# ScalarE issues the down loads of experts 1 to 28 on its own queue, in place of SyncE

## The chip, the core and the metric

One core of a Trainium2 chip runs the whole kernel. The time is the device time of one execution in microseconds (us), from start to end; of several runs the median counts. The engines are TensorE (PE; PEld is its weight load), VectorE (DVE), ScalarE (ACT), GpSimd (POOL) and SyncE (SP). SyncE, ScalarE and GpSimd can issue transfers, each on a queue of its own: in the profile q1 is SyncE's, q10 ScalarE's, q0 GpSimd's. All queues are served by the same 16 transfer engines.

## The reference, cut to what matters

The reference is one layer of a hybrid encoder on 272 tokens (16 meta tokens and a sequence of 256), with a model width of 1024, in float32. First comes a mixer of two kinds of attention (not touched here), then a mixture of 32 experts, of which each token takes 4:

```
gu = xb @ w_gate_up[e] + b_gate_up[e]                 # 1024 x 2048 per expert
act = x_glu * sigmoid(1.702 * x_glu) * (x_lin + 1)    # both halves clamped at 7
yb = act @ w_down[e] + b_down[e]                      # 1024 x 1024 per expert
out[token] += gate * yb
```

A final norm is applied, and the 256 tokens of the sequence are the output. Every expert has tokens, so all expert weights are read: 8.4 MB of gate and up rows and 4.2 MB of down rows for each of 32 experts, 403 MB in all.

## The kernel before, in words

**Loads and slots.** The mixer takes the first 250 us. The experts follow in one pass (more passes are possible if an expert has more than 64 tokens). An expert's weights come in three loads of 4 MB: two for the gate and up matrix (four of eight row groups each) and one for the down matrix. The 96 loads of a pass have numbers 0 to 95. There are four slots of 4 MB in SBUF, two in the tensor `arena` and two in `ring`; load n goes to slot n mod 4 (`eslot`, L413). The order of the numbers is that of use by TensorE: gate and up of expert 0 (loads 0, 1), gate and up of expert 1 (2, 3), down of expert 0 (4), gate and up of expert 2 (5, 6), down of expert 1 (7), and so on. So the down load of expert x is load 3x + 4, and its slot was last used by load 3x, the second gate and up load of expert x.

**Who issues them.** SyncE issues every load, in the order of the numbers. Loads 0 to 3 go ahead, while the mixer still ends. Before every other load it waits until TensorE has used its slot: TensorE adds 1 to the semaphore `wide_used` of the slot after each quarter of a load, and `slot_free` (L483) waits for all four. Loads 4 to 11 (`first_refill`, L487) go in quarters of 1 MB, each as soon as its own quarter of the slot is used. Loads 12 to 92 are whole (`whole_load`, L495): 12 to 83 in a loop of 6 turns of 12 loads, then one by one. Loads 93 to 95 (`last_loads`, L500) go in quarters again, of load 95 only the first half, since the other half (`kept`) was loaded long before. A load that lands adds 16 to `wide_loaded` of its slot; of a quartered load the last quarter does so, and the first three add to `part_loaded`.

**TensorE.** It waits in `arrived` (L1676) for the load, and for loads 4 to 11 also for `part_loaded`. It works in pairs of experts (`expert_pair`, L1738): gate and up products of the odd expert (L1696), with the transposes of the expert before it between the two loads (L1673), the transpose of the gated pick (L1706), the down products of the even expert (L1712), the scatter into PSUM (L1732), for the next pair the gather of its tokens (L1600), then the same with the next even expert's gate and up and the odd expert's down rows, without a gather. The last pair is written out (`last_pair`, L1776).

**ScalarE.** Its own `expert_pair` (L771) does for each pair: sigmoid; `rows_out` (L749), the copy of the gate and up products out of PSUM, for which it waits with `slot_done` (L396) until TensorE has used the second gate and up load of the expert; `pick_out` (L761), the copy of the gated pick; `down_out` (L766), the copy of the down products; and the same again for the second expert. It issues no loads of expert weights. Its queue carries four small loads near 246 us (L736 to L738) and at the end the store of the second tile (L820), while SyncE stores the first (L571).

Of the kernel before, what the change touches and what calls it, by code (L numbers as in the profile page):

```python
# [65 lines left out]
DN_ROWS = 2 * GU_ROWS  # L66
EWIDTH = GU_ROWS * 2 * D
ESLOT = 2 * NSLOT * SLOT // EWIDTH
GU_LOADS = CH // GU_ROWS
# [5 lines left out]
UNROLL = 2  # L75
# [4 lines left out]
REFILL_END = 3 * ESLOT  # L80
LOAD_TURNS = (PASS_LOADS - ESLOT - REFILL_END) // TURN_LOADS
BIAS_TURN = 3

LAST_READ = [("mid", 2)] * 2 + [("ka", 1), ("ka", 3), ("qa", 1), ("qa", 3)] + [("va", 2)] * 2 \
    + [("gate", 2 * m + 1) for m in range(8)] + [("ba", 3)] * 2 + [("bb", 3)] * 2 \
# [49 lines left out]
def build(nc, x, meta, w_in, b_forget, w_uq, w_uk, w_uv, w_qidx, kln_g, kln_b, w_a, w_b, w_out,  # L135
# [10 lines left out]
    with ctx:  # L146
# [254 lines left out]
        def cols(first, n):  # L401

            return slice(first, first + n) if isinstance(first, int) else bass.ds(first, n)
# [9 lines left out]
        def eslot(k):  # L413

            home, n = divmod(k % ESLOT, ESLOT // 2)
            return (ring if home else more)[:, n * EWIDTH:(n + 1) * EWIDTH]
# [23 lines left out]
        def _(sp):  # L440
# [45 lines left out]

            def first_refill(base):  # L487

                for idx in range(ESLOT, REFILL_END):
                    for q in range(QUARTERS):  # L490
                        sp.wait_ge(wide_used[idx % ESLOT], base + QUARTERS * (idx // ESLOT - 1) + q + 1)
                        quarter_of(idx, rows_of(idx - GU_LOADS, 1), q,
                                   wide_loaded[idx % ESLOT] if q == QUARTERS - 1 else part_loaded[idx % ESLOT])

            def whole_load(idx, base, e0):  # L495

                slot_free(idx, base)
                sp.dma_start(eslot(idx), rows_of(idx - GU_LOADS, e0)).then_inc(wide_loaded[idx % ESLOT], 16)
# [13 lines left out]
            def whole_pass(b):  # L512

                base = b * (QUARTERS * PASS_USES)
                if not isinstance(b, int):
                    base = sp.snap(base)
                first_refill(base)
                with sp.Fori(0, LOAD_TURNS) as j:
                    turn = j * (QUARTERS * TURN_USES) + base
                    if not isinstance(b, int):  # L520
                        turn = sp.snap(turn)
                    for o in range(TURN_LOADS):
                        whole_load(REFILL_END + o, turn, j * (2 * UNROLL) + 1)
                for idx in range(REFILL_END + LOAD_TURNS * TURN_LOADS, PASS_LOADS - ESLOT):
                    whole_load(idx, base, 1)
                last_loads(base)

# [77 lines left out]
        def _(sc):  # L605
# [143 lines left out]
            def rows_out(tb, o, home):  # L749

                slot_done(sc, tb, o)
                sc.activation(gl.rearrange("q (b j p) -> q b j p", p=P, j=DN_ROWS),  # L752
                              banks(home, home + 2).rearrange("q (b p j) -> q b j p", p=P, j=DN_ROWS),
                              ACT.Copy).then_inc(s_gl, 1)

            def sigmoid(x):

                sc.wait_ge(s_glu, x + 1)
                sc.activation(sg, glu, ACT.Sigmoid, scale=1.702).then_inc(s_sig, 1)  # L759

            def pick_out(x, home):  # L761

                sc.wait_ge(s_pgf, x + 1)
                sc.activation(pickgT, bank[home][:, 0:2 * P], ACT.Copy).then_inc(s_pgt, 1)
# [3 lines left out]
                slot_done(sc, tb, o)  # L768
                sc.activation(yr, bank[1], ACT.Copy).then_inc(s_y, 1)  # L769

            def expert_pair(tb, u, last):  # L771
                a = tb * (2 * UNROLL) + 2 * u
                o = 2 * EXPERT_LOADS * u
                sigmoid(a)
                rows_out(tb, o + 1, 2)
                pick_out(a, 7)
                if last:
                    sigmoid(a + 1)
                down_out(tb, o + 2)
                if not last:  # L780
                    sigmoid(a + 1)
                    rows_out(tb, o + 4, 2)
                pick_out(a + 1, 0 if last else 7)
                down_out(tb, o + 3 if last else o + 5)

            with sc.Fori(0, n_pass) as b:
                rows_out(sc.snap(b * TURNS), -1, 6)
                sc.wait_ge(s_btf, b + 1)
                sc.activation(biasT[:].rearrange("p (h n) -> p h n", h=2),
                              banks(0, 2).rearrange("p (h n) -> p h n", h=2)[:, :, 0:CH * EXPERTS],  # L790
                              ACT.Copy).then_inc(s_bT, 1)
                with sc.Fori(0, BIAS_TURN) as j:
                    tb = sc.snap(b * TURNS + j)
                    for u in range(UNROLL):
                        expert_pair(tb, u, False)
                sc.wait_ge(s_gzf, b + 1)
                sc.activation(gT, bank[1][0:EXPERTS, 0:2 * P], ACT.Copy).then_inc(s_gT, 1)
                with sc.Fori(BIAS_TURN, TURNS - 1) as j:
                    tb = sc.snap(b * TURNS + j)
                    for u in range(UNROLL):  # L800
                        expert_pair(tb, u, False)
                tb = sc.snap(b * TURNS + (TURNS - 1))
                expert_pair(tb, 0, False)
                expert_pair(tb, 1, True)
# [454 lines left out]
        def _(pe):  # L1259
# [416 lines left out]
            def arrived(tb, o):  # L1676

                idx = GU_LOADS + o
                pe.wait_ge(wide_loaded[idx % ESLOT], tb * (16 * TURN_USES) + 16 * (idx // ESLOT + 1))
                if ESLOT <= idx < REFILL_END and parts[0] is not None:  # L1680
                    pe.wait_ge(part_loaded[idx % ESLOT], parts[0] + 48 * (idx // ESLOT))

            def gate_up(tb, o, e, home, fresh, between):

# [48 lines left out]
                                 yr[n * CAP:(n + 1) * CAP, :], start=True, stop=True)  # L1733
                    ins.then_inc(s_sc, 1)

            ahead, parts = [None], [None]

            def expert_pair(tb, u):  # L1738
                g = tb * UNROLL + u
                x = tb * (2 * UNROLL) + 2 * u  # L1740
                o = 2 * EXPERT_LOADS * u

                def first_features():

                    pe.wait_ge(s_pkg, g + 1)
                    features(x)

                def second_features():

                    pe.wait_ge(s_acc[0], x + 1)  # L1750
                    features(x + 1)

                gate_up(tb, o, 1, 2, None, first_features)
                pick_rows(x, 0)
                down(tb, o + 2, x)
                scatter(x)
                pe.wait_ge(s_pick, g + 1)
                gather(0)
                gather(1)
                gate_up(tb, o + 3, 0, 2, g * 2 + 2, second_features)  # L1760
                for t in range(2):
                    pe.wait_ge(s_acc[t], x + 1)
                pick_rows(x + 1, 1)
                down(tb, o + 5, x + 1)
                scatter(x + 1)
# [60 lines left out]
            with pe.Fori(0, n_pass) as b:  # L1826
                x = pe.snap(b * EXPERTS)
                ahead[0] = pe.snap(b * 16 + 16)
                fine = pe.snap(b * (48 * (REFILL_END // ESLOT - 1)))
                gate_up(pe.snap(b * TURNS), -GU_LOADS, 0, 6, x, None)  # L1830
                pe.wait_ge(s_bias, 32)
                bias_features()
                parts[0] = fine
                with pe.Fori(0, BIAS_TURN) as j:
                    tb = pe.snap(b * TURNS + j)
                    for u in range(UNROLL):
                        expert_pair(tb, u)
                parts[0] = None
                for t in range(2):
                    ins = tr(bank[1][0:EXPERTS, t * P:(t + 1) * P], gz[:, t, :], ident)  # L1840
                ins.then_inc(s_gzf, 1)
                pe.wait_ge(s_bdn, 16)
                for t in range(2):
                    pe.wait_ge(s_acc[t], x + 4 * BIAS_TURN)
                pe.wait_ge(s_gT, b + 1)
                for t in range(2):
                    for n in range(2):
                        ins = mm(bank[4 + 2 * t + n], gT[:, t * P:(t + 1) * P], bdn[:, n * 512:(n + 1) * 512],
                                 start=True, stop=True)
                    ins.then_inc(s_bm, 1)  # L1850
                with pe.Fori(BIAS_TURN, TURNS - 1) as j:
                    tb = pe.snap(b * TURNS + j)
                    for u in range(UNROLL):
                        expert_pair(tb, u)
                tb = pe.snap(b * TURNS + (TURNS - 1))
                expert_pair(tb, 0)
                last_pair(tb, b)
                for t in range(2):
                    pe.wait_ge(s_acc[t], x + EXPERTS)
                    pe.wait_ge(s_ba[t], b + 1)  # L1860
# [51 lines left out]
```

## Time and profile before

| | us |
|---|---|
| median of three runs | 1174.15 (1173.03 to 1175.33) |
| profiled execution | 1176.58 |
| its span, from the first to the last instruction | 1174.8 |
| TensorE busy | 1109.2 (94%) |
| VectorE busy | 336.3 (29%) |
| ScalarE busy | 206.3 (18%) |
| GpSimd busy | 14.5 (1%) |
| share of the 16 transfer engines taken by q1 | 87.4% |
| share taken by q0, by q10 | 0.6%, 0.4% |

A busy share is over the whole span. The strips of the page cut the span into 40 slices of 29.4 us. The chain that ended last is given as 67% TensorE and 27% transfers. A whole load's median time from issue to landing is between 27.7 and 29.8 us by kind; this is queueing and transfer together.

### The profile page before, as it was taken

The page shows a single profiled execution, that of the slowest core. Times are in us where ns is not written, and L with a number is a line of the kernel's source. Part 1 is how long each engine was busy: PE and PEld are TensorE (multiplying, and loading weights), DVE is VectorE, ACT ScalarE, POOL GpSimd, SP SyncE. Part 2 cuts the span into 40 slices and gives each one's busy share as a digit, 9 for nine tenths or more (in the row PEclk, how much of TensorE's full clock was granted, in tenths as well). Part 3 has the DMA queues.
Part 4 walks back from the last instruction along what each step waited for, and adds up shares of the span by engine and source line. Part 5 has one row for each costly group of instructions (what it writes and reads, how often), then busy time and mean ns, then how long its engine had stood idle before and what let it go on. Part 6 is the DMA issues. An engine that isn't in the chain of part 4 may idle for free.

```text
span 1174.8 us, 13591 instructions
## 1 busy us (share of the span) xinstructions
PE 1109.2 (94%) x5490; PEld 528.0 (45%) x5490; DVE 336.3 (29%) x773; ACT 206.3 (18%) x361; POOL 14.5 (1%) x27
## 2 busy tenths in 40 slices
PE   8999999999999999989899999898989899999897
PEld 6878888553443434333434343334333433343333
DVE  2256442131232222313222322122222222222223
ACT  2437772031001000100000100000000010100012
POOL 3010000000000000000000000000000000000000
PEclk9999999999999999999989999999999999999999
DMA  9813237759999999999999999999999999999992
GB/s 303 279 37 110 106 109 285 322 203 423 421 431 432 433 434 431 430 432 433 434 431 429 429 429 433 436 431 430 431 433 435 431 431 430 432 436 429 432 415 99
DMA packets 39734, 433.66 MB, mean 369 GB/s; under 512 B 3144, under 2 KB 19682, under 8 KB 23188
## 3 DMA queue, kind: packets, MB, share of 16 engines
q1 hardware_dynamic: 38144, 429.45, 87.4%
q0 software_dynamic: 960, 2.30, 0.6%
q10 hardware_dynamic: 596, 1.45, 0.4%
q8 instruction: 23, 0.38, 0.1%
q14 instruction: 11, 0.09, 0.0%
HBM read 432.13 MB, written 1.05 MB: 369 GB/s over the span
## 4 chain that ended last, share of the span: by engine, by line
PE 67%; DMA 27%; DVE 2%; ACT 2%; issue 1%; SPq 0%; ACTq 0%; DVEq 0%
PE psum L1696 24%; PE psum L1712 13%; DMA arena<-in_w_down 12%; DMA ring<-in_w_down 10%; PE psum L1550 4%; PE psum L1600 4%; PE psum L1732 3%; PE psum L1350 2%; PE psum L1529 2%; DMA ring<-in_w_gate_up 2%; DMA arena<-in_w_gate_up 2%; PE psum L1569 2%; PE psum L1673 2%; PE psum L1790 1%; ACT arena L769 1%; PE psum L1310 1%
## 5 line engine op out<-in xcount | busy, mean ns | idle before, releaser
L1696 PE MATMUL psum<-ring,arena 128*64 128x512 f32 x992 | 221.5, 599 | 3.9 <-DMA ring<-in_w_gate_up 3.9
L1696 PE MATMUL psum<-arena 128*64 128x512 f32 x992 | 220.4, 597 | 1.5 <-DMA arena<-in_w_gate_up 1.5
L1193 DVE TENSOR_TENSOR h<-h,psum 128x1024 f32<-128x1024 f32 x64 | 75.3, 1218 | 423.0 <-PE psum L1732 423.0
L1696 PEld LDWEIGHTS psum<-ring,arena 128*64 128x64 f32 x992 | 69.3, 138 | 138.8 <-issue 137.1
L1712 PE MATMUL psum<-ring,arena 128*64 128x512 f32 x528 | 121.9, 615 | 9.6 <-DMA ring<-in_w_down 7.2
L1696 PEld LDWEIGHTS psum<-arena 128*64 128x64 f32 x992 | 68.7, 137 | 135.8 <-issue 132.5
L1712 PE MATMUL psum<-arena 128*64 128x512 f32 x496 | 115.1, 618 | 11.1 <-DMA arena<-in_w_down 11.0
L1173 DVE TENSOR_TENSOR arena<-psum,biasT 128x512 f32<-128x512 f32 x64 | 44.0, 687 | 196.5 <-PE psum L1673 196.5
L759 ACT ACTIVATE arena<-arena 128x512 f32<-128x512 f32 x32 | 20.2, 630 | 413.7 <-DVE arena L1177 413.7
L1732 PE MATMUL psum<-arena 64*128 64x512 f32 x256 | 63.6, 611 | 25.2 <-ACT arena L769 25.2
L1712 PEld LDWEIGHTS psum<-ring,arena 128*64 128x64 f32 x528 | 40.3, 141 | 80.0 <-issue 80.0
L1712 PEld LDWEIGHTS psum<-arena 128*64 128x64 f32 x496 | 35.9, 141 | 79.3 <-issue 69.6
L752 ACT ACTIVATE arena<-psum 128x1024 f32<-128x1024 f32 x32 | 32.8, 1024 | 180.4 <-PE psum L1696 175.2
L1600 PEld LDWEIGHTS psum<-arena 128*128 128x128 f32 x512 | 58.4, 192 | 12.1 <-issue 12.1
L1600 PE MATMUL psum<-arena 128*128 128x128 f32 x512 | 61.4, 278 | 0.0
L1550 PE MATMUL psum<-arena,ring 128*128 128x256 f32 x256 | 60.5, 379 | 0.0
L769 ACT ACTIVATE arena<-psum 128x512 f32<-128x512 f32 x32 | 19.1, 597 | 226.0 <-PE psum L1712 226.0
L1732 PEld LDWEIGHTS psum<-arena 64*128 64x128 f32 x256 | 24.8, 186 | 65.6 <-issue 65.6
L1550 PEld LDWEIGHTS psum<-arena,ring 128*128 128x128 f32 x256 | 46.2, 190 | 5.6
L1673 PEld LDWEIGHTS psum<-kst,arena 128*128 128x128 f32 x256 | 27.4, 141 | 26.1 <-issue 25.2
L836 DVE TENSOR_TENSOR arena<-psum,vT 128x512 f32<-128x512 f32 (+1 forms) x42 | 28.4, 681 | 36.9 <-PE psum L1600 23.7
L1673 PE MATMUL psum<-kst,arena 128*128 128x128 f32 x256 | 35.0, 280 | 0.8 <-ACT arena L752 0.8
(232 smaller groups left out, 767.9 us busy)
## 6 DMA issues: line engine op xcount, KB each, us to landing
arena<-in_w_gate_up SPq DMA_DIRECT2D x29, 4096.0 KB, 29.8
ring<-in_w_gate_up SPq DMA_DIRECT2D x28, 4096.0 KB, 29.8
arena<-in_w_down SPq DMA_DIRECT2D x14, 4096.0 KB, 29.0
ring<-in_w_down SPq DMA_DIRECT2D x13, 4096.0 KB, 27.7
arena<-in_w_gate_up SPq DMA_DIRECT2D x16, 1024.0 KB, 15.4
ring<-in_w_in SPq DMA_DIRECT2D x14, 1024.0 KB, 12.1
ring<-in_w_down SPq DMA_DIRECT2D x14, 1024.0 KB, 16.4
ring<-in_w_gate_up SPq DMA_DIRECT2D x8, 1024.0 KB, 15.4
```

What stands on the lines that cost most here:

```text
L752: sc.activation(gl.rearrange("q (b j p) -> q b j p", p=P, j=DN_ROWS), banks(home, home + 2).rearrange("q (b p j) -> q b j p", p=P, j=DN_ROWS),
L769: sc.activation(yr, bank[1], ACT.Copy).then_inc(s_y, 1)
L836: return v.tensor_tensor(dst, src, vec.unsqueeze(2).broadcast_to([P] + cols), ALU.mult)
L1173: return v.tensor_tensor(dst.rearrange("p (m j) -> p m j", m=8), src, bias[:, m:m + 8, cols(e, 1)].broadcast_to([P, 8, CAP]), ALU.add)
L1193: v.tensor_tensor(half, half, banks(4 + 2 * t, 6 + 2 * t), ALU.add).then_inc(s_acc[t], 1)
L1350: ins = mm(job_bank(name)[:, 0:width], win(s)[:, c, k * P:(k + 1) * P], xnT[:, c, cols:cols + width], start=c == 0, stop=c == CH - 1)
L1550: ins = mm(job_bank(name)[:, 0:SEQ], win(8 + m // 2)[:, c, (m % 2) * P:(m % 2 + 1) * P], xnT[:, c, META:KEYS], start=c == 0, stop=c == CH - 1)
L1600: ins = mm(bank[k][:, c * P:(c + 1) * P], hs[:, t, (4 * k + c) * P:(4 * k + c + 1) * P], pick[:, t, :], start=t == 0, stop=t == 1)
L1673: ins = tr(bank[4 + m // 4][:, (m % 4) * P:(m % 4 + 1) * P], gl[:, m * P:(m + 1) * P], ident)
L1696: ins = mm(bank[home + n][h * CAP:(h + 1) * CAP, :], xg[:, c, e * CAP:(e + 1) * CAP], eslot(idx)[:, (2 * j + h) * D + n * 512:(2 * j + h) ...
L1712: ins = mm(bank[1][n * CAP:(n + 1) * CAP, :], act[:, c * CAP:(c + 1) * CAP], w[:, n * 512:(n + 1) * 512], start=first, stop=last)
L1732: ins = mm(bank[4 + 2 * t + n], pickgT[n * CAP:(n + 1) * CAP, t * P:(t + 1) * P], yr[n * CAP:(n + 1) * CAP, :], start=True, stop=True)
```

## The change

`BY_SCALAR` names loads 7, 10, 13, ... 88: the down loads of experts 1 to 28. SyncE leaves them out wherever it issued them. ScalarE issues each one, whole, right after the `rows_out` that has waited for the last use of its slot. Down loads of experts 0, 29, 30 and 31 stay with SyncE. Since loads 7 and 10 are now whole, the quartered loads of the start (`FINE`) are 4, 5, 6, 8, 9 and 11, and TensorE counts `part_loaded` accordingly. Slots, order of use and semaphores for arrival are the same.

```diff
+LOOP_EXPERTS = 2 * UNROLL * (TURNS - 1)
+BY_SCALAR = [GU_LOADS + EXPERT_LOADS * x + 2 for x in range(1, LOOP_EXPERTS + 1)]
+FINE = [idx for idx in range(ESLOT, REFILL_END) if idx not in BY_SCALAR]
...
-                for idx in range(ESLOT, REFILL_END):
+                for idx in FINE:
...
                     for o in range(TURN_LOADS):
+                        if REFILL_END + o in BY_SCALAR:
+                            continue
                         whole_load(REFILL_END + o, turn, j * (2 * UNROLL) + 1)
                 for idx in range(REFILL_END + LOAD_TURNS * TURN_LOADS, PASS_LOADS - ESLOT):
+                    if idx in BY_SCALAR:
+                        continue
                     whole_load(idx, base, 1)
...
+            def down_load(o, e):
+
+                sc.dma_start(eslot(GU_LOADS + o), w_dn[0, cols(e, 1), :, :].rearrange("e (p j) n -> p (e j n)", j=DN_ROWS)
+                             ).then_inc(wide_loaded[(GU_LOADS + o) % ESLOT], 16)
...
-            def expert_pair(tb, u, last):
+            def expert_pair(tb, u, last, pair=None):
                 a = tb * (2 * UNROLL) + 2 * u
                 o = 2 * EXPERT_LOADS * u
                 sigmoid(a)
                 rows_out(tb, o + 1, 2)
+                if pair is not None:
+                    down_load(o + 5, pair + 1)
                 pick_out(a, 7)
...
                 if not last:
                     sigmoid(a + 1)
                     rows_out(tb, o + 4, 2)
+                    if pair is not None:
+                        down_load(o + 8, pair + 2)
                 pick_out(a + 1, 0 if last else 7)
...
-                        expert_pair(tb, u, False)
+                        expert_pair(tb, u, False, j * (2 * UNROLL) + 2 * u)
...
-                if ESLOT <= idx < REFILL_END and parts[0] is not None:
-                    pe.wait_ge(part_loaded[idx % ESLOT], parts[0] + 48 * (idx // ESLOT))
+                if idx in FINE and parts[0] is not None:
+                    home = [n for n in FINE if n % ESLOT == idx % ESLOT]
+                    pe.wait_ge(part_loaded[idx % ESLOT], parts[len(home) - 1] + 48 * (home.index(idx) + 1))
```

## Rows read from the trace of the kernel before

**Rows 1.** The page: busy tenths of the transfer engines in 40 slices of the span.
```profile
DMA  9813237759999999999999999999999999999992
```

**Rows 2.** Windows: us, busy time (instructions) of each engine, TensorE clock, DMA share, GB/s.
```profile
330.00:475.00 145.00, 141.06 (x706) 56.30 (x706) 39.86 (x64) 14.54 (x22) 0.00 (x0) 1.00 1.01 432
475.00:1150.00 675.00, 628.59 (x3020) 245.49 (x3018) 171.88 (x285) 61.66 (x97) 0.00 (x0) 0.98 1.00 431
```

**Rows 3.** Waits of TensorE, 470 to 1175 us: us in total, times, longest.
```profile
PE psum L1712 <- DMA arena<-in_w_down: 11.0, 5, 2.3
PE psum L1712 <- DMA ring<-in_w_down: 7.2, 4, 2.4
```

**Rows 4.** Timeline of TensorE near the end: start us, length, instruction, idle before it.
```profile
1079.64 7.09 PE L1696 MATMUL psum<-ring,arena 128*64 128x512 f32 x32 [1.66 <-DMA ring<-in_w_gate_up]
1086.65 0.44 PE L1706 MATMUL psum<-kst,arena 128*128 128x128 f32 x2
1089.28 7.09 PE L1712 MATMUL psum<-arena 128*64 128x512 f32 x32 [2.19 <-DMA arena<-in_w_down]
...
1118.51 7.09 PE L1712 MATMUL psum<-ring,arena 128*64 128x512 f32 x32 [0.17 <-DMA ring<-in_w_down]
```

**Rows 5.** Last quarters of loads 6 and 11, load 91: issue, then time to landing.
```profile
L481 SPq DMA_DIRECT2D ring<-in_w_gate_up x1: 328/328/328, 276.0 to 276.0; - x1
...
DMA to landing us min/median/max: 14.0/14.0/14.0
...
L481 SPq DMA_DIRECT2D ring<-in_w_gate_up x1: 328/328/328, 320.4 to 320.4; - x1
...
DMA to landing us min/median/max: 19.3/19.3/19.3
...
L498 SPq DMA_DIRECT2D ring<-in_w_down x1: 328/328/328, 1086.8 to 1086.8; - x1
...
DMA to landing us min/median/max: 31.6/31.6/31.6
```

**Rows 6.** ScalarE's timeline; queues (rows, MB, share) in 246.8 to 249, 249 to 252.
```profile
245.97 2.13 ACT L731 ACTIVATE arena<-h,st 128x1024 f32<-128x1024 f32 x1 [0.23 <-DVE st L1077]
245.97 0.80 ACTq L736 DMA_DIRECT2D arena<-in_b_gate_up  x2
...
q1 hardware_dynamic: 52, 0.85, 90.4%
...
q10 hardware_dynamic: 251, 0.83, 98.3%
```

**Rows 7.** The stores: issues; queues in 1171.2 to 1172.4, then in 1172.5 to 1173.1.
```profile
1170.23 0.39 ACTq L820 DMA_DIRECT2D out<-arena  x1
1170.26 1.00 SPq L571 DMA_DIRECT2D out<-arena  x2
...
1171.42 0.34 ACTq L820 DMA_DIRECT2D out<-arena  x1
...
q10 hardware_dynamic: 114, 0.23, 51.1%
q1 hardware_dynamic: 120, 0.23, 51.1%
...
q1 hardware_dynamic: 112, 0.23, 97.1%
q10 hardware_dynamic: 13, 0.01, 3.9%
```

**Rows 8.** GpSimd's issue; queues in 16 to 18 us, then in 22 to 23.
```profile
14.11 0.58 POOL L584 DMA_DIRECT2D bfor<-in_b_forget  x1 [11.60 <-DMA ring<-in_w_in]
...
q1 hardware_dynamic: 689, 0.70, 110.4%
...
q0 software_dynamic: 73, 0.28, 75.0%
q1 hardware_dynamic: 76, 0.08, 24.1%
```

More of the change, by code:

```diff
@@ L800, in _ @@
                     for u in range(UNROLL):
-                        expert_pair(tb, u, False)
+                        expert_pair(tb, u, False, j * (2 * UNROLL) + 2 * u)
                 tb = sc.snap(b * TURNS + (TURNS - 1))
@@ L1734, in scatter @@
                     ins.then_inc(s_sc, 1)
-            ahead, parts = [None], [None]
+            ahead, parts = [None], [None, None]
             def expert_pair(tb, u):
@@ L1828, in _ @@
                 ahead[0] = pe.snap(b * 16 + 16)
-                fine = pe.snap(b * (48 * (REFILL_END // ESLOT - 1)))
+                fine = [pe.snap(b * (48 * n)) for n in (1, 2)]
                 gate_up(pe.snap(b * TURNS), -GU_LOADS, 0, 6, x, None)
@@ L1832, in _ @@
                 bias_features()
-                parts[0] = fine
+                parts[:] = fine
                 with pe.Fori(0, BIAS_TURN) as j:
```

## The prediction

> **What bounds the kernel now.** First the strip over the span: the transfer engines are full in every slice from the tenth on, to the last but one [rows 1]. The windows say how full: 432 GB/s at a share of 1.01 from 330 to 475 us, 431 GB/s at 1.00 up to 1150, with TensorE busy for 628.6 of the 675 us of the second stretch [rows 2]. A load is 4.194 MB, so it takes 4.194 / 432 = 9.71 us of all engines. TensorE is the smaller load, and what ends its waits is the arrival of down rows, nine times, 18.2 us in all [rows 3]. So from about 260 us to the end of the loads the time is the number of bytes over the rate, as long as the queue never runs dry. Last, the end of the chain: TensorE waits 2.19 us for the down rows of expert 28 (load 88) and begins on them at 1089.28; it meets load 91 at 1118.51 after only 0.17 us of waiting and goes on without a wait for weights to the end of the span at 1174.8 [rows 4]. That start at 1089.28, and the one at 1118.51 behind it, are what the change has to move if it is to move the time; the 56.3 us behind 1118.51 are TensorE, VectorE and the store.
>
> Terms below are against the profiled execution, 1176.58 us (span 1174.8, and 1.8 around it); the median of the runs is 1174.15, so I take the differences found here from the median.
>
> **The change, part by part.**
>
> *Issuing 28 down loads from ScalarE.* SyncE loses 28 issues of 0.33 us, which lay in waits for slots: worth nothing. ScalarE gains 28 issues of 0.34 to 0.39 us [rows 7], some 10 us in all. Each stands behind the copy of the gate and up rows and before the copy of the gated pick. ScalarE's queue can issue while its engine still runs: a load was issued at 245.97, in the same moment in which an activation of 2.13 us began [rows 6]. So the issue fits beside the copy ahead of it. If it did not, the pick copy would come 0.4 us late; it is needed only behind the down products, which take 7.09 us [rows 4], and all that follows on ScalarE waits for TensorE anyway. Bounds 0 and 0.4 us on a step with over 6 us of cover: 0.
>
> *When the load is issued.* Its slot is that of the second gate and up load of the expert in hand, and ScalarE waits for that very use before its copy. SyncE waited for the same event. Moved by 0.1 us or so, with more than two loads outstanding: 0.
>
> *SyncE's order.* It no longer waits for those slots before it goes on to the next load, but the next load's slot comes free later still (it is the slot of the down rows used after). Nothing is issued earlier: 0.
>
> *The first two (loads 7 and 10) whole and not in quarters.* They leave at about 284.1 and 313.1, when the last quarter of the slot is free; before, their first quarters left 5 us sooner. Does the queue run dry meanwhile? The last quarter of load 6 left at 276.0 and landed 14.0 us later, at 290.0 [rows 5]: 5.9 us of work stand ahead at 284.1. The last quarter of load 11 left at 320.4 and landed at 339.7, so five quartered loads took 49.7 us, 9.94 each, and load 9 landed near 319.8: 6.7 us of cover at 313.1. No gap. There is a small gain: 9.94 against 9.71 us is 0.23 us for three boundaries more, or 0.077 us for each; two loads with three boundaries fewer give -0.46 us. Bounds -0.5 and 0; as the queue bounds all that follows, I take -0.4.
>
> *The waits of TensorE* are the same in number or fewer, none on the path.
>
> *Two queues in place of one.* This is the term that decides, and it depends on how an engine serves a row of SyncE's queue (q1) and a row of ScalarE's (q10) when both have work. At the issue of a down load, the queue holds 2.25 loads ahead of it: one took 31.6 us to land, 3.25 loads of 9.71 [rows 5], and a load is 8 rows of 32 KB for each of the 16 engines, so 18 rows an engine. If these go first, the order of arrival is that of before and the term is 0. If the two queues alternate at once, the down load takes half of the rate and the gate and up loads needed sooner come late.
>
> Three places show queues side by side. (a) ScalarE issued loads at 245.97 and after; in the whole stretch 246.8 to 249.0 q1 had 52 rows and q10 none, and q10 came when q1 was through [rows 6]. (b) At the end both queues issue a store within 0.03 us: from 1171.2 to 1172.4 they have 120 and 114 rows, in alternation; that also puts the delay from issue to first row under 1 us. But ScalarE's second store, issued at 1171.42, behind SyncE's second (before 1171.26), gets 13 rows in 1172.5 to 1173.1 where q1 gets 112: it stands behind it whole, 8 rows an engine [rows 7]. (c) GpSimd's queue (q0), with a load issued at 14.11, has no row in 16 to 18, while q1 alone moves 689 (43 an engine); then, with a long backlog on both, they have 73 and 76 rows in 22 to 23 [rows 8]. What reached the engines first goes first, to a depth of some 40 rows, and only beyond it do the queues alternate. 18 rows lie within 40. So I take 0, with (b) and (c) as the nearest rows: the down load on its own queue stays behind what SyncE issued before it.
>
> The Trainium skill, page "DMA: Bandwidth & Descriptors", section "Queues, rings and completion order", states that each engine takes turns between the queue rows it has work for, a packet at a time. By that rule the down load would share from the start, and the sum would be that of the first rival below. The rows at 249 and at 1173 speak against it, those at 1171.2 and at 22 for it.
>
> **Sum:** 0 + 0 + 0 - 0.4 + 0 = -0.4 us: 1173.7 as the median.
>
> **Rivals.**
>
> *The queues share at once (slower).* Then a down load takes 2 x 9.71 = 19.4 us from its issue and is there long before its use, a whole expert later; the second gate and up load, being last of its queue, lands only after the down load issued before it was needed (the sum of both queues up to there has to pass). So the wait of TensorE moves from the down rows to load 87, and load 87 lands when 88 loads have come, at 1089.2, and not at 1079.6 [rows 4]. Behind its arrival stand 7.0 us of products and 0.4 of a transpose (1079.64 to 1087.1 before), so the products on load 88 begin at 1096.6 and not at 1089.28: +7.3 us. From there to 1118.51 TensorE had no slack before (29.2 us with 0.17 us of waiting), and all the later loads are there: the whole 7.3 us reach the end. Against it the -0.4: 1174.15 + 6.9 = 1181.0. It decides as soon as the second gate and up load is held back by over 7.2 us of the 9.7 a down load needs; with less, the chain at 1089.28 still waits for load 88 and the time stays. For it: the alternation in (b) and late in (c). Against it: (a), and the second store in (b). Chance 0.25.
>
> *The boundaries vanish (faster).* A boundary between two loads costs 0.077 us by the quarters. With the two queues served in order but separate, the end of a load on one might pass under the rows of the other: 28 loads with two such boundaries, 56 x 0.077 = 4.3 us, and 0.4: 1169.4. It counts as faster once each boundary gives back over 0.035 us ((2.35 - 0.4) / 56). For it: 9.94 against 9.71. Against it: the share is 1.00 to 1.01 already with one queue, so the profile shows no hole to fill. Chance 0.10.
>
> *The rate falls (slower).* Two streams from two places of memory, with rows of both in flight, could cost rate: 0.3% of the 890 us of loads is 2.7 us, 1% is 8.9: 1177 to 1183. No row shows such a loss; in (b) the two together take a share of 102.2% of the engines [rows 7]. Chance 0.05, within the slower ones.
>
> **How the numbers follow.** The forecast, no change of order, has 0.60. A fifth of a percent, 2.35 us, is about what a measurement of this kernel can tell from no change. The forecast ends within it. Faster: the 0.10 of the boundaries. Slower: 0.25 for sharing, less 0.02 in which too little is held back to count, and 0.05 for the rate, 0.28. Same: the 0.60 and those 0.02, 0.62. The range has to take in sharing, at 1181.0, since it holds more than 2 in 10; above it 1182 leaves out a rate that falls by 1%. Below, 1171 takes in the gain of the quarters and a part of the boundaries. The forecast's own range is 1172.5 to 1175.5.
>
> **What would show it.** Right: down loads on q10 take some 29 to 31 us to land, as before; TensorE's waits for weights stay with the down rows, near 18 us; the products on load 88 begin at about 1089. Wrong by sharing: down loads land in about 20 us, gate and up loads in 27 to 33, the waits stand before the second gate and up load, and TensorE waits for no down rows. Wrong by boundaries: the rate from 475 to 1150 is over 432 GB/s with the waits where they were. Wrong by the rate: it is under 430. The quarters: a share below 1.00 between 284 and 320 us would be a gap that I have put at nothing.

## The result and the profile after

The change makes the kernel slower: 1181.36 us as the median of four runs (1181.20 to 1184.08) against 1174.57 (1173.03 to 1175.33), a ratio of 1.0064 with a 95% interval of 1.0051 to 1.0078. That is +6.8 us; I had forecast -0.4 and held 1181.0 for the first rival, sharing of the engines. The profiled execution took 1181.20 us, with a span of 1179.4.

The page of the changed kernel (busy time of TensorE first, then the strip of the transfer engines, then three queues with rows, MB and share of 16 engines) answers to [rows 1]:

```profile
PE 1113.0 (94%) x5490; PEld 527.8 (45%) x5490; DVE 336.3 (29%) x773; ACT 206.3 (17%) x361; POOL 14.4 (1%) x27
...
DMA  9813237769999999999999999999999999999991
...
q1 hardware_dynamic: 33248, 312.01, 63.7%
q10 hardware_dynamic: 4628, 118.89, 23.5%
q0 software_dynamic: 960, 2.30, 0.6%
```

The 28 loads are on q10, and the engines are as full as before. The windows, as in [rows 2], say the same of the rate: 432 and 430 GB/s where it was 432 and 431. The bytes do not move more slowly.

```profile
330.00:475.00 145.00, 135.86 (x671) 54.08 (x671) 38.70 (x63) 14.53 (x22) 0.00 (x0) 0.99 1.01 432
475.00:1150.00 675.00, 631.91 (x3025) 244.29 (x3022) 170.81 (x283) 61.02 (x96) 0.00 (x0) 0.98 1.00 430
```

What changed is what TensorE waits for. Its waits for weights from 250 us on (us in total, times, longest), first those for gate and up rows before the change, which go beside the down rows of [rows 3], then all of the changed kernel:

```profile
PE psum L1696 <- DMA ring<-in_w_gate_up: 3.9, 3, 1.7
PE psum L1696 <- DMA arena<-in_w_gate_up: 1.5, 1, 1.5
...
PE psum L1713 <- DMA ring<-in_w_gate_up: 16.1, 7, 2.7
PE psum L1713 <- DMA arena<-in_w_gate_up: 11.8, 5, 2.5
```

Before, TensorE waited 5.4 us for gate and up rows and 18.2 for down rows. Now down rows are never waited for; gate and up rows are, twelve times and 27.9 us, each time at the second load of an expert. The issues on the page (KB each, median us from issue to landing) tell why: a down load now lands in 23.4 us, where the medians before were 27.7 and 29.0 for down loads and 29.8 for gate and up loads. Gate and up loads land sooner too, in 26.5 us: the median of 57 loads doesn't show what happens to load 87, which took 31.4 (below).

```profile
arena<-in_w_gate_up SPq DMA_DIRECT2D x29, 4096.0 KB, 26.5
ring<-in_w_gate_up SPq DMA_DIRECT2D x28, 4096.0 KB, 26.3
ring<-in_w_down ACTq DMA_DIRECT2D x14, 4096.0 KB, 23.4
arena<-in_w_down ACTq DMA_DIRECT2D x14, 4096.0 KB, 23.5
```

And the end, TensorE's timeline, against [rows 4]:

```profile
1086.77 7.09 PE L1713 MATMUL psum<-ring,arena 128*64 128x512 f32 x32 [2.71 <-DMA ring<-in_w_gate_up]
1093.79 0.44 PE L1723 MATMUL psum<-kst,arena 128*128 128x128 f32 x2
1094.16 7.09 PE L1729 MATMUL psum<-arena 128*64 128x512 f32 x32
...
1123.15 7.09 PE L1729 MATMUL psum<-ring,arena 128*64 128x512 f32 x32
```

The last wait for weights is now for load 87, until 1086.77; before, it was for load 88, but for 0.17 us in front of load 91. Behind it stand the products on load 87 and a transpose, so those on load 88 begin at 1094.16 and not at 1089.28. From there on TensorE never waits for weights (load 91 at 1123.15 follows without one), so the delay reaches the end.

The mixer ahead of the experts takes a little longer or shorter in each execution: SyncE issued the first quarter of load 4 at 255.51 us before and at 254.62 after. The table counts from that issue to the start of the products on load 88; this takes the mixer out and is what I compare between profiles. The medians are of runs made in four groups, each beside its own runs of the kernel before: 1174.57 us for the changed kernel, 1175.38 for the next four rows, 1173.86 for GpSimd and the filled wait, 1174.80 for the two rows on whole loads.

| kernel | load 4 issued | products on load 88 | between | against before | median, us |
|---|---|---|---|---|---|
| before | 255.51 | 1089.28 | 833.77 | | 1174.57 |
| changed | 254.62 | 1094.16 | 839.54 | +5.8 | 1181.36 |
| 85 and 88 back on SyncE | 252.60 | 1086.44 | 833.84 | +0.1 | 1175.74 |
| only 88 on ScalarE | 252.76 | 1095.51 | 842.75 | +9.0 | 1182.70 |
| only 85 on ScalarE | 253.86 | 1090.34 | 836.48 | +2.7 | 1176.05 |
| 88 in quarters on ScalarE | 253.59 | 1112.70 | 859.11 | +25.3 | 1200.44 |
| 88 on GpSimd | 253.89 | 1097.20 | 843.31 | +9.5 | 1183.56 |
| 7 and 10 whole, all on SyncE | 252.80 | 1086.15 | 833.35 | -0.4 | 1174.91 |
| 6 to 11 whole, all on SyncE | 253.01 | 1085.99 | 832.98 | -0.8 | 1175.17 |
| before, wait for 88 filled | 253.78 | 1088.14 | 834.36 | +0.6 | 1174.84 |

The last row says how finely this column can be read. Its loads are those of the kernel before, and yet it is 0.6 us later already at load 87, ahead of the first filling product (1078.50 less 253.78, against 1079.64 less 255.51). So differences of 0.6 us between two single profiles mean nothing.

**Where the queues meet.** ScalarE's timeline around the issue of load 88, and behind it the queues' rows in 1066.1 to 1069 and in 1070 to 1080:

```profile
1065.91 1.02 ACT L759 ACTIVATE arena<-psum 128x1024 f32<-128x1024 f32 x1 [7.71 <-PE psum L1713]
1066.05 0.34 ACTq L765 DMA_DIRECT2D arena<-in_w_down  x1
1066.83 0.38 ACT L776 ACTIVATE arena<-psum 128x256 f32<-128x256 f32 x1
```

```profile
q1 hardware_dynamic: 46, 1.18, 94.5%
...
q10 hardware_dynamic: 69, 2.26, 52.4%
q1 hardware_dynamic: 64, 2.10, 48.8%
```

The issue runs beside the copy, as costed. For 3 us after it q1 is alone; the first row of q10 starts at 1069.2. Then the two have 69 and 64 rows, half of the rate each, though two loads of q1 stood ahead. Load 87 was issued at 1055.3 and landed 31.4 us later; load 88 was issued 10.8 us behind it and landed after 23.4 us, at 1089.4. The row of load 87's issue and its time to landing:

```profile
L501 SPq DMA_DIRECT2D ring<-in_w_gate_up x1: 328/328/328, 1055.3 to 1055.3; - x1
...
DMA to landing us min/median/max: 31.4/31.4/31.4
```

### The profile page after: what moved, and what is told of

It is laid out like the page before. It is cut to its first block, busy times and chain, and to the rows that moved or that the text cites. A ratio compares the mean times of both kernels' runs of the same rounds, so it can differ in the third digit from the quotient of the medians.

```text
span 1179.4 us, 13598 instructions
## 1 busy us (share of the span) xinstructions
PE 1113.0 (94%) x5490; PEld 527.8 (45%) x5490; DVE 336.3 (29%) x773; ACT 206.3 (17%) x361; POOL 14.4 (1%) x27
## 4 chain that ended last, share of the span: by engine, by line
PE 67%; DMA 28%; DVE 2%; ACT 1%; issue 1%; SPq 0%; ACTq 0%; DVEq 0%
PE psum L1713 26%; DMA ring<-in_w_gate_up 16%; PE psum L1729 13%; DMA arena<-in_w_gate_up 11%; PE psum L1566 4%; PE psum L1749 4%; PE psum L1366 2%; PE psum L1545 2%; PE psum L1585 2%; PE psum L1616 2%; PE psum L1326 1%; PE psum L1807 1%; ACT arena L781 1%; PE psum L1689 1%; PE psum L1528 1%
## 5 line engine op out<-in xcount | busy, mean ns | idle before, releaser
L1749 PE MATMUL psum<-arena 64*128 64x512 f32 x256 | 63.6, 611 | 25.2 <-ACT arena L781 25.2
L1689 PEld LDWEIGHTS psum<-kst,arena 128*128 128x128 f32 x256 | 27.4, 141 | 26.1 <-issue 25.1
## 6 DMA issues: line engine op xcount, KB each, us to landing
arena<-in_w_gate_up SPq DMA_DIRECT2D x29, 4096.0 KB, 26.5
ring<-in_w_down ACTq DMA_DIRECT2D x14, 4096.0 KB, 23.4
```

What stands on the lines that cost most here:

```text
L1689: ins = tr(bank[4 + m // 4][:, (m % 4) * P:(m % 4 + 1) * P], gl[:, m * P:(m + 1) * P], ident)
L1749: ins = mm(bank[4 + 2 * t + n], pickgT[n * CAP:(n + 1) * CAP, t * P:(t + 1) * P], yr[n * CAP:(n + 1) * CAP, :], start=True, stop=True)
```

## The experiments

Theory A: the order of arrival changes, since the queues share the engines, and all that costs is that load 87, the last gate and up load with a wait, comes late. Rival B: each load on a second queue costs a little. Theories C and D are on how the queues share: by rows, one of each in turn whatever its size (C), or by bytes (D).

### Two loads back on SyncE

```diff
-BY_SCALAR = [GU_LOADS + EXPERT_LOADS * x + 2 for x in range(1, LOOP_EXPERTS + 1)]
+BY_SCALAR = [GU_LOADS + EXPERT_LOADS * x + 2 for x in range(1, LOOP_EXPERTS - 1)]
```

(and the last turn of ScalarE's loop written out, without its second pair's loads)

> The changed kernel, but loads 85 and 88 (the down rows of experts 27 and 28) go back to SyncE; ScalarE keeps 26 of its 28. Theory A (only the place of the last second gate and up load ahead of the end counts: load 87 is held back by load 88 on the other queue, and TensorE has no slack behind it): load 88 comes last again, the products on it begin near 1089, and the time is that of before, 1174.6, within 1.5 us. Rival B (every load on the second queue costs a little, by rate or by clock): 26/28 of the loss of 6.8 us stays, 1180.9.

Measured: 1175.74 us, ratio 1.0009 (0.9997 to 1.0021). The waits of TensorE in it are still those of the changed kernel for most of the pass:

```profile
PE psum L1716 <- DMA ring<-in_w_gate_up: 12.9, 5, 3.3
PE psum L1716 <- DMA arena<-in_w_gate_up: 8.8, 4, 2.3
```

26 loads on the second queue, nine waits on the gate and up rows, and no loss that can be measured: at most 2.5 us by the interval, where B wanted 6.3. B is out. In the profiled execution the last of the nine waits ended at 998.11, and the products on load 88 began 833.84 us after the issue of load 4, as before (table). One part of theory A is not seen here: it had load 88 come last again. It was issued at 1061.0, landed 24.4 us later, at 1085.4, and TensorE began on it only at 1086.44, when it was through with the products ahead. So the equal time shows that the lateness of the moved waits is made up by then, not that load 88 set the time.

### Only load 88, only load 85

```diff
+BY_SCALAR = [GU_LOADS + EXPERT_LOADS * 28 + 2]
...
```

(27 in the second kernel; ScalarE issues it in the last turn of its loop, written out, and no other load)

> The kernel before, but ScalarE issues load 88 alone. Theory A: load 88 shares with 86 and 87 from about 3 us after its issue, load 87 lands some 7 us later than before, the products on load 88 begin 4 to 7 us later, and the time is 4 to 7 us over before, 1179 to 1181.5, from one load of the 28. Rival B: 1/28 of the loss, 1174.8.

> The kernel before, but ScalarE issues load 85 alone, one expert earlier. Theory A: load 84 comes late and TensorE waits before it, but loads 86 to 88 come in order again and load 88 ends the wait near 1089 as before: 1174.6, within 1 us. If only some load near the end has to be on the other queue, it would cost as much as load 88 does, 4 to 7 us. Rival B: 1174.8.

Load 88 alone: 1182.70 us, ratio 1.0066 (1.0049 to 1.0083). One load of the 28 costs what all cost. Load 85 alone: 1176.05, ratio 1.0012 (1.0002 to 1.0021), 0.7 us by the medians of ten and 19 runs. TensorE's timeline with only load 88:

```profile
1072.99 8.72 PE L1714 MATMUL psum<-ring,arena 128*64 128x512 f32 x32 [6.98 <-DMA ring<-in_w_gate_up]
1086.43 8.78 PE L1714 MATMUL psum<-ring,arena 128*64 128x512 f32 x32 [3.69 <-DMA ring<-in_w_gate_up]
1095.51 7.09 PE L1730 MATMUL psum<-arena 128*64 128x512 f32 x32
```

and the window 1086 to 1090 of it (columns as in [rows 2]):

```profile
1086.00:1090.00 4.00, 3.57 (x10) 1.18 (x12) 0.44 (x1) 0.00 (x0) 0.00 (x0) 0.57 0.99 426
```

Here load 88 landed 24.5 us after its issue at 1055.8, at 1080.3, long before load 87 at about 1086.4. That is the full case of the rival. The products on load 87 took 8.78 us and not 7.09, with a granted clock of 0.57 in that window after 3.69 us without work, so part of them ran at 1.2 GHz: +1.7 us. Without these, 9.0 is 7.3 us, the figure of the rival. The medians differ by 7.3 us too, with the clock's part in them; how often it falls in the other executions isn't known. With load 85 alone there are two smaller waits, and load 88 follows at 1090.34 without one:

```profile
1046.90 8.78 PE L1714 MATMUL psum<-ring,arena 128*64 128x512 f32 x32 [4.60 <-DMA ring<-in_w_gate_up]
1057.74 7.09 PE L1714 MATMUL psum<-arena 128*64 128x512 f32 x32 [1.03 <-DMA arena<-in_w_gate_up]
1065.12 7.09 PE L1730 MATMUL psum<-arena 128*64 128x512 f32 x32
1090.34 7.09 PE L1730 MATMUL psum<-arena 128*64 128x512 f32 x32
```

TensorE is late by what it lost there and makes up part of it in the waits that it would have had: load 84 was waited for until 803.9 us after the issue of load 4, where the products on it began at 797.2 before, 6.7 us less; of that the waits of 1.66 and 2.19 us for loads 87 and 88 [rows 4] fall away, and +2.7 is left. I had expected load 88 to end the wait as before, and it does not in this profile. By the medians it is 0.7, and 2.5 at most by the interval; the profiled execution, 1177.39 us, is among the slowest of its ten.

### Load 88 in four quarters

```diff
...
+                for q in range(QUARTERS):
+                    part = slice(q * QWIDTH, (q + 1) * QWIDTH)
+                    sc.dma_start(eslot(GU_LOADS + o)[:, part], rows[:, part]
+                                 ).then_inc(wide_loaded[(GU_LOADS + o) % ESLOT] if q == QUARTERS - 1 else s_q88, 16)
...
```

(TensorE also waits for `s_q88`, the first three quarters)

> As the run with load 88 alone on ScalarE, but in four quarters, so its rows are 8 KB and not 32 KB. If the engines take a row of each queue in turn (theory C), SyncE's rows of 32 KB leave it a fifth of the rate as long as SyncE's queue has work: load 88 lands only when loads 86, 87, 89 and 90 have all but passed, 45 us or more after its issue, TensorE waits for it until 1105 to 1116, and the time is 15 to 27 us over before, near 1195. If the queues share by bytes (rival D), it is that of the run with load 88 whole, 1179 to 1181.5.

Measured: 1200.44 us, ratio 1.0212 (1.0193 to 1.0232), 25.1 us by the medians: C. The queues in 1064 to 1104:

```profile
q1 hardware_dynamic: 477, 13.63, 79.4%
q10 hardware_dynamic: 478, 3.52, 21.0%
```

477 rows against 478, and a share of 79.4% against 21.0%: a row of each in turn, whatever its size. (109 of these rows are under 512 B; by MB over row size the rows with data are 416 and 430.) It starts so at once: from 1063 to 1064.5 q1 had 17 rows and q10 21. TensorE waits for load 88 until 1112.70, within the 1105 to 1116 expected:

```profile
1112.70 8.70 PE L1734 MATMUL psum<-arena 128*64 128x512 f32 x32 [21.84 <-DMA arena<-in_w_down]
```

### Load 88 on GpSimd's queue

```diff
...
+            idx = BY_SCALAR[0]
+            pool.wait_ge(wide_used[idx % ESLOT], QUARTERS * (idx // ESLOT))
+            pool.dma_start(eslot(idx), w_dn[0, 28:29, :, :].rearrange("e (p j) n -> p (e j n)", j=DN_ROWS)
+                           ).then_inc(s_p88, 16)
...
```

(TensorE waits for `s_p88` in place of the slot's semaphore)

> The kernel before, but load 88 alone is issued by GpSimd, which has nothing else to do then, on its own queue at the same event. If what counts is that the load is on another queue than the loads it shares the engines with (theory A), the loss is that of load 88 on ScalarE's queue, perhaps a little less since GpSimd's first rows come later after the issue: 1179 to 1182. If it is something of ScalarE or its queue, the time is that of before, 1174.8.

Measured: 1183.56 us, ratio 1.0080 (1.0064 to 1.0095), 1.6 us above the upper end of the range I gave. It is the queue, not ScalarE. The issue was at 1059.32, and q0 had its first row at 1063.0 to 1063.2, some 3.7 us later. The wait before load 87 is longer still, and its products again ran in part at the lower clock:

```profile
1088.46 8.45 PE L1718 MATMUL psum<-ring,arena 128*64 128x512 f32 x32 [7.96 <-DMA ring<-in_w_gate_up]
1096.84 0.44 PE L1728 MATMUL psum<-kst,arena 128*128 128x128 f32 x2
1097.20 7.09 PE L1734 MATMUL psum<-arena 128*64 128x512 f32 x32
```

### The loads issued 8 us later

```diff
                 rows_out(tb, o + 1, 2)
-                if pair is not None:
-                    down_load(o + 5, pair + 1)
                 pick_out(a, 7)
...
                 down_out(tb, o + 2)
+                if pair is not None:
+                    down_load(o + 5, pair + 1)
```

(the second load of the pair likewise)

> The changed kernel, but ScalarE issues each down load some 8 us later, after the copy of the down products and not after the copy of the gate and up products. Theory A: the down load takes rate from the other queue later, so load 87 comes earlier than in the changed kernel and load 88 lands just behind it; the wait goes back to the down rows or lies on both, and most of the loss goes: 1175 to 1178. Rival B: all 28 loads are still on the second queue, 1181.4. Rival E (a later issue only makes loads late): over 1181.4.

Measured: 1229.76 us, ratio 1.0470 (1.0443 to 1.0497). This missed: I had thought that the later load would only stand further back, and had "over 1181.4" for rival E alone, in which a later issue only makes loads late. Its waits, and the windows 475 to 1200 and 712 to 716 us:

```profile
PE psum L1729 <- DMA arena<-in_w_down: 31.6, 13, 5.6
PE psum L1729 <- DMA ring<-in_w_down: 29.1, 12, 5.9
```

```profile
475.00:1200.00 725.00, 653.64 (x3064) 255.14 (x3062) 174.08 (x289) 61.65 (x97) 0.00 (x0) 0.95 0.95 404
...
712.00:716.00 4.00, 4.00 (x20) 1.25 (x16) 0.00 (x0) 0.00 (x0) 0.00 (x0) 1.00 0.37 156
```

The rate falls to 404 GB/s, since the queues run dry: a share of 0.37 in a window just after a long wait. TensorE waits for the down load until 707.02, the others land meanwhile, and no slot comes free while it waits: SyncE issued one load at 692.97 and the next at 716.30, behind the products on the down load. The 25.2 MB of a pair take 62.3 us at 404 GB/s and 58.2 at 432; 14 pairs make some 57 us of that, and 55 were measured. So the loads have to be issued at once. The changed kernel issues them so, and its share from 330 to 1150 us is 1.00 to 1.01.

### The quartered loads, and a filled wait

```diff
+                    if idx not in FINE:
+                        whole_load(idx, base, 1)
+                        continue
```

(all on SyncE; `FINE` without 7 and 10, and without 6 to 11)

> The kernel before, all loads on SyncE, but loads 7 and 10 whole, as the change makes them. My prediction's term: -0.4 us (six boundaries of 0.077 us fewer), so 1174.2. Rival: the later start of these loads costs what the fewer boundaries give, 0 to +1 us.

> The kernel before, all loads on SyncE, but loads 6 to 11 whole; only 4 and 5 stay in quarters. By the same price, 18 boundaries fewer are -1.4 us: 1173.2, if the queue does not run dry near 276 (load 6 would leave then, and load 5 landed at 280.1). If it runs dry there, 0 or above.

Measured: 1174.91 us, ratio 0.9994 (0.9985 to 1.0003), and 1175.17, ratio 1.0003 (0.9993 to 1.0013). In the profiles the products on load 88 begin 0.4 and 0.8 us earlier than before (table); the terms that I had put down are 0.4 and 1.4, and 0.6 us is what this column can be off by. The runs show no gain for either. So the price of a boundary, 0.077 us, isn't confirmed by the times, though the rate from 284 to 320 us is a little higher: 421 GB/s before, 430 and 426 in these two. In both profiles the products on load 88 took 8.78 us, before 7.09:

```profile
1086.15 8.78 PE L1717 MATMUL psum<-arena 128*64 128x512 f32 x32 [2.18 <-DMA arena<-in_w_down]
```

That led to the last run, in which TensorE has small products to do during the wait for load 88:

```diff
+                if warm[0] and o == 2:
+                    for _ in range(8):
+                        mm(bank[0][:, 0:P], ident, ident, start=True, stop=True)
                 arrived(tb, o)
```

> The kernel before, with eight products of the identity with itself into an unused PSUM bank, some 1.8 us, in front of TensorE's wait for load 88. In two of three profiles of kernels with all loads on SyncE the products on load 88 ran 8.78 us and the granted clock was 0.57 to 0.62 in the 4 us around their start, in the third they took 7.09 at 1.00. If idling in the wait costs the 1.7 us, filling it gives 7.09 us each time and 0.5 to 1.7 us less in the median: 1173.1 to 1174.3. If not, or if the filling delays the products, the time is that of before or up to 1 us more.

Measured: 1174.84 us, ratio 1.0007 (0.9998 to 1.0016): no gain.

```profile
1088.14 7.09 PE L1712 MATMUL psum<-arena 128*64 128x512 f32 x32 [0.39 <-DMA arena<-in_w_down]
...
1117.37 7.09 PE L1712 MATMUL psum<-ring,arena 128*64 128x512 f32 x32 [0.17 <-DMA ring<-in_w_down]
```

The products ran at 7.09 us, and load 91 was still waited for. The median is 1.0 us above that of the kernel before in the same group, and the interval takes in no change. How often the other executions run these products at the lower clock isn't known, so why no median moved stays open.

## Why the prediction was wrong

**The step that failed is "Two queues in place of one", put at 0.** From three places I took that what reached the engines first goes first, "to a depth of some 40 rows", and that "18 rows lie within 40". The lead is no number of rows. The first row of the second queue on busy engines came 3.1 us after the issue of load 88 in the changed kernel (1066.05 to 1069.2), 3.3 with load 88 alone (1055.8 to 1059.1), 3.1 with it in quarters (1059.9 to 1063.0), and 2.6 and 3.4 us for loads 7 and 10, with rows of 8 KB ahead. In [rows 6] it is 245.97 to 249.0, again 3 us. In [rows 8] it is 14.11 to 18.0, 3.9 us, in which q1 alone moved 1377 rows of 1 KB, 86 an engine, and not the 43 that the prediction took from the second half of it; load 88 on the same queue had 3.7. In [rows 7] the second store, issued at 1171.42, has its first rows behind 1173.0, 1.6 us later (some of its 13 rows are the last of the first store), behind 8 rows an engine of 2 KB. 18 rows of 32 KB are 22 us of work. All three places are leads of 1.6 to 3.9 us, read as depths in rows and carried over to rows up to 32 times as large. From then on the queues take turns, as [rows 8] showed for a long backlog. What makes up the 3 us stays open.

The rule that I set aside is that of the Trainium skill, page "DMA: Bandwidth & Descriptors", section "Queues, rings and completion order": each engine takes turns between the queue rows it has work for, a packet at a time. The trace agrees with the turns, behind that delay: 69 and 64 rows in 10 us.

**The first rival had the mechanism and the size.** It gave +7.3 us at load 88 and 1181.0 in all; measured are 9.0 with 1.7 of it from the clock (load 88 alone), and 1181.36. In the changed kernel the profile shows +5.8, since load 88 landed 2.7 us after load 87 (1089.4 against 1086.7) and so had not held it back in full. The medians differ by 6.8, and the 1.0 us between the two isn't explained; that 1181.36 lies so near 1181.0 is in part luck. The rival's signs were met (down loads faster, waits in front of the second gate and up load, none for down rows) but for one: gate and up loads landed in 26.5 us by the median, not in 27 to 33. I gave it 0.25, and only because of it did my range go up to 1182.

**A slip in the rival.** It said that load 87 must be held back by over 7.2 us before the time moves. By its own rows it is 2.2: the products on load 87 and the transpose ended at 1087.1, and load 88 came at 1089.28. The runs bear this out. Counted from the issue of load 4, the wait for load 87 ended at 824.1 before, at 832.2 in the changed kernel and at 833.7 with load 88 alone; 8.0 and 9.5 us less 2.2 are 5.8 and 7.3. So the 0.02 that was moved to "same" for a load held back too little had no ground in the rows.

**Steps that held, and one not shown.** The issue beside the copy cost nothing. The queue did not run dry at 284 or 313 us: by the sign that I had set, a share below 1.00 in 284 to 320, there are 0.89 in 296 to 300 and 0.84 in 316 to 320, but these stand beside 1.08 and 1.20, and the whole stretch has 1.01 at 426 GB/s, where it had 1.01 at 421. The rate stayed, so neither the boundaries nor a loss of rate moved the time. The gain of the quarters, -0.4, is within the noise, in the profiles and in the runs: not shown. And the start on load 88 was the place that counted, as one load alone showed; [rows 3] left out the four waits for gate and up rows, 5.4 us, so "what ends its waits is the arrival of down rows" held for most of them only.

## What to carry to other kernels

A load on a second queue overtakes what the first queue has not begun: on full engines it took its turn here, row by row, after some 3 us. In a stream whose order is the order of use, this trades an early load that nobody needs for a late one that somebody waits for; here it was free only where the waiting engine still had slack behind it. And a depth seen in small rows must be turned into time or bytes before it is used for large ones.

## What the runs showed of the hardware that was not expected

Taking turns goes by rows, not by bytes: rows of 8 KB against rows of 32 KB had 21.0% against 79.4% of the engines with 478 and 477 rows, so cutting a load into quarters on a second queue made it land over 50 us after its issue, and cost 25 us in all. Second, when ScalarE's queue started on busy engines, its first row came 2.6 to 3.4 us after the issue, with 8, 16 or 32 KB rows ahead, and GpSimd's 3.7 and 3.9 us after, while two stores issued together on idle engines had rows within 1 us. Third, a down load issued 8 us late cost 55 us over 28 loads, through slots that stayed taken, though each load still took only 22 us to land.
